# A merged attention and delta-rule stage: first keys and values on another DMA queue, first key block halved, first three query tiles in another order

## The reference, cut to what matters

```python
s = einsum(q_nope, k_nope) + einsum(q_pe, k_pe)        # per query block of 128
p = softmax(where(k_pos <= q_pos, s * scale, -inf))
o = einsum(p, v)
decay = exp(where(causal, g[..., :, None] - g[..., None, :], -inf))
```

## Time and profile before

| | us |
|---|---|
| median of three runs | 2585.17 |
| lowest, highest | 2581.58, 2592.66 |
| time of the profiled execution | 2578.27 |
| its span | 2576.6 |
| TensorE busy in the span | 2331.9 (91%) |
| first DMA of the merged stage issued | at 698.24 |

### The profile page before, as it was taken

The page is one execution under the profiler, slowest core; times in us unless marked ns, Lnnn a source line. Parts: engine busy times, 40 slices in busy tenths (PEclk is TensorE's granted clock), DMA queues, the critical chain, the costliest instruction groups (busy, mean ns, idle before and its releaser), DMA issues. The chain is left out here.

```text
span 2576.6 us, 47589 instructions
## 1 busy us (share of the span) xinstructions
PE 2331.9 (91%) x17494; PEld 1339.2 (52%) x17495; DVE 1074.2 (42%) x2440; ACT 910.1 (35%) x2283; POOL 392.4 (15%) x630
## 2 busy tenths in 40 slices
PE   6999999999688999999999999699985999999990
PEld 2545545455356666666666667355543444444440
DVE  2433334333345665665666566224345222222223
ACT  2263462734545554554545554111110011010112
POOL 1000000000110000000000010133321222222224
PEclk8999999999879999999999999899987999999995
DMA  9112121110353213121221112833321879999787
GB/s 335 72 65 70 52 78 54 56 54 32 107 141 105 75 53 94 56 82 49 80 69 65 51 33 95 294 126 111 131 90 33 238 193 307 273 323 303 225 237 287
DMA packets 187896, 334.49 MB, mean 130 GB/s; under 512 B 19724, under 2 KB 119719, under 8 KB 184503
## 3 DMA queue, kind: packets, MB, share of 16 engines
q1 hardware_dynamic: 173878, 281.51, 32.3%
q0 software_dynamic: 13824, 50.34, 8.1%
HBM read 242.36 MB, written 89.44 MB: 129 GB/s over the span
## 5 line engine op out<-in xcount | busy, mean ns | idle before, releaser
L706 PE MATMUL pV<-mod_rows_then_work,w_in_sb 128*128 128x512 f32 x768 | 341.3, 598 | 4.7 <-DMA w_in_sb<-in_w_in_dram 4.7
L2066 PE MATMUL hidden_ps<-w,keys_values_then_all 128*128 x752 | 331.5, 594 | 1.0 <-SPq L1938 1.0
L1140 ACT ACTIVATE probs<-scores,neg_max 128x512 f32<-128x512 f32 (+3 forms) x320 | 199.5, 624 | 345.6 <-DVE neg_max L1265 228.5
L1417 PE MATMUL scores<-keys_values_then_all,queries 96*128 96x512 f32 (+3 forms) x640 | 309.9, 567 | 7.2 <-DMA keys_values_then_all<-kp_d 7.2
L706 PEld LDWEIGHTS pV<-mod_rows_then_work,w_in_sb 128*128 128x128 f32 x768 | 145.0, 191 | 178.2 <-issue 177.5
L2066 PEld LDWEIGHTS hidden_ps<-w,keys_values_then_all 128*128 128x128 f32 x752 | 143.2, 191 | 181.5 <-issue 181.5
L1715 PE MATMUL out_ps<-keys_values_then_all 128*128 128x512 f32 x512 | 226.2, 600 | 2.5 <-ACT keys_values_then_all L1580 2.5
L1422 PE MATMUL bank<-ident,probs 128*128 128x128 f32 x1088 | 188.7, 290 | 7.0 <-ACT probs L1140 6.7
L1265 DVE TENSOR_REDUCE neg_max<-scores 128x1 f32<-128x512 f32 x192 | 132.2, 688 | 131.7 <-PE scores L1417 131.1
L1434 PE MATMUL outT_ps<-probs_T,keys_values_then_all 128*64 128x128 f32 x2176 | 160.0, 287 | 27.3 <-issue 23.1
L1996 ACT ACTIVATE keys_values_then_all<-hidden_ps 128x256 f32<-128x256 f32 x47 | 18.0, 384 | 455.5 <-PE hidden_ps L2066 455.5
(11 more groups left out here) (368 smaller groups left out, 3317.3 us busy)
## 6 DMA issues: line engine op xcount, KB each, us to landing
w<-in_w_dram SPq DMA_DIRECT2D x64, 1024.0 KB, 10.3
w_sb<-in_w_dram SPq DMA_DIRECT2D x32, 1024.0 KB, 14.4
w_mod_rows<-in_w_mod_dram SPq DMA_DIRECT2D x16, 1024.0 KB, 5.0
kqv<-qkv_d SPq DMA_DIRECT2D x16, 768.0 KB, 4.3
mod_rows_then_work<-in_w_mod_dram SPq DMA_DIRECT2D x4, 2048.0 KB, 14.9
x_in<-in_x_dram SPq DMA_DIRECT2D x16, 512.0 KB, 4.2
qkv_d<-l_out SPq DMA_DIRECT2D x32, 256.0 KB, 2.3
keys_values_then_all<-y_d SPq DMA_DIRECT2D x16, 512.0 KB, 4.9
```

The lines of the kernel that those rows point to most:

```text
L706: last = pe.matmul(pV[n % 2][:], win[:, k, QKV0 + c * P:QKV0 + (c + 1) * P], hT[:, s % 2, k, :], start=(k == 0), stop=(k == ND - 1))
L1140: act.activation(prob[:, e, 0:w].rearrange("p t k -> p (t k)"), pS[e][:, 0:w * P], ACT.Exp, scale=-1.0, bias=nmin[:, i % 2, h, b:b + 1], a ...
L1417: pe.matmul(pS[e][:, 0:w * P], qT[:, i % 2, slot(h)], kT[:, 4 * b:4 * b + w, slot(h), :], start=True, stop=True).then_inc(s_ready, 1)
L2066: last = pe.matmul(pH[par][:], xT[par][:, k], m.w13[:, ds(slot, 1), k].rearrange("p s n -> p (s n)"), start=(k == 0), stop=(k == ND - 1))
```

## The change

`TILE` begins 1, 3, 0 instead of 3, 0, 1. `KV` gets a border at tile 2. The two load helpers take the issuing engine; groups 0 and 1 (tiles 0 and 1, tiles 2 and 3) are issued by ScalarE ahead of its table load, the others by SyncE as before. SyncE issues the first decay rows ahead of the first q, k, v.

```diff
-TILE = [3, 0, 1] + list(range(4, NT)) + [2]
+TILE = [1, 3, 0] + list(range(4, NT)) + [2]
-    KV = [0, 4, 8, 12, NT]
+    KV = [0, 2, 4, 8, 12, NT]
+        def load_k(eng, n):
+            t, end = KV[n], KV[n + 1]
+            eng.dma_start(kT[0:NOPE, t:end].rearrange("p t (e b) k -> p (t e) (b k)", e=2),
+                          m.kn_d[t * P:end * P, :].rearrange("(e p) n -> p e n", p=NOPE)).then_inc(k_loaded[n], 16)
+            for i in range(t, end):
+                eng.dma_start(kT[NOPE:, i], m.kp_d[i * ROPE:(i + 1) * ROPE, :].unsqueeze(1).to_broadcast([ROPE, AH, P])
+                              ).then_inc(k_loaded[n], 16)
+
+        def load_v(eng, n):
+            t, end = KV[n], KV[n + 1]
+            eng.dma_start(v[:, t:end], m.v_d[t * P:end * P, :].rearrange("(t p) n -> p t n", p=P)).then_inc(v_loaded[n], 16)
...
+            load_g(0)
             load_kq(0)
-            load_g(0)
             load_q(0)
-            load_k(0)
-            load_v(0)
             load_q(1)
...
-                    for s in range(1, len(KV) - 1):
+                    for s in range(2, len(KV) - 1):
                         if i == max(0, KV[s] - 5):
-                            load_k(s)
-                            load_v(s)
+                            load_k(sp, s)
+                            load_v(sp, s)
...
         @block.scalar
         def _(act):
             wait = waiter(act)
+            for n in range(2):
+                load_k(act, n)
+                load_v(act, n)
             act.preload_act_table_set("natural_log_exp_and_others")
```

More of the change, by code:

```diff
@@ L920, in _ @@
             wait = waiter(sp)
[L922 to L932, removed]
             def load_q(i):
```

## The result

Over 22 runs each, the changed kernel takes 2592.74 us (median) and the kernel before 2587.98 us: ratio 1.0019, 95% interval 1.001 to 1.0028. It is 4.9 us slower, well within the 0.5% that the prediction took as no change, but on the other side of the forecast of 7.8 us less, and 0.7 us above the range. The range was built on the median of three runs, 2585.17, and with the ratio on that base the time would be 2590.1, inside it: the direction is what failed, for the interval leaves out 1. The profiled execution after took 2600.46 us, its span is 2598.7. The two profiled executions are not typical of their kernels: that of before lies 9.7 us under its median over 22 runs, that of after 7.7 us over. So of the 22 us between the two traces only 4.9 are the kernels'.

What follows compares the result with a forecast made beforehand. TensorE was taken to bound the stage's long middle, with waits and low clock in its first 102 us. Gains of 2.4 + 2.9 + 2.5 = 7.8 us took 2585.17 to 2577.4, range 2566 to 2592 (8 in 10).

Steps and rivals of the forecast that it cites:

- The opening: Start of the merged stage: first mask at 713.4 instead of 715.82, 2.4 us gained (0.2 to 3.9).
- I take the middle, 705.3: Opening: q, k, v land at 705.3, between 703.1 (ScalarE takes nothing from SyncE) and 707.5 (equal bytes).
- the late bound: Opening: with equal bytes for both queues, q, k, v land at 707.5 and 0.2 us are gained.
- The rows' place ahead of q, k, v gives nothing by itself: Opening: the 2.12 us wait for decays goes, but q, k, v take its place.
- ScalarE's issues: Opening: eight DMA issues take 5.4 us, then a 1.28 us table load; hidden with 0.6 us to spare.
- rival (c): Opening: ScalarE gets stuck issuing, from 1.25 us an issue on; mask 6.5 to 8.7 us later, 2592 to 2594; chance 0.07.
- First combine: First tile's combine no longer waits behind ScalarE's copies: 2.9 us gained (0 to 3.3).
- Clock: Low clock from 745 to 760, behind the first combine's wait, may go: 2.5 us gained (0 to 7.5).
- The new order: Merged stage: 697 of 1664 list places hold another step, same work; 6 us either way through the clock.
- rival (d): Merged stage: the 697 moved steps cost, 6 us, at 2591; chance 0.10 on the losing side alone.
- (a): Opening and combines: q, k, v share equally, the combine's wait reappears elsewhere; 0.2 us gained, 2585; chance 0.25.
- signs of being wrong: ScalarE's issues averaging over 1.25 us, first mask later than 715.8, or windows from 800 on differing more than the opening.

Runs made afterwards that it cites:

- e3: The changed kernel with q, k, v ahead of the decay rows on SyncE again; ratio to before 1.0005.
- e12: The kernel before with the first keys and values (six DMAs) issued by ScalarE, nothing else moved; ratio to before 1.0024.
- e11: The changed kernel with q, k, v ahead of the rows and ScalarE waiting for them to land before its eight loads; ratio to before 1.003.
- e1: The kernel before with the tile order 1, 3, 0 alone, all loads as before; ratio to before 0.9995.
- e10: The kernel before with the first tile's combine moved ahead of the delta-rule steps with ScalarE's copies; ratio to before 0.9992.
- e5: The changed kernel with q, k, v ahead of the rows and ScalarE issuing only the first group's keys; ratio to before 1.0.
- e6: New tile order and halved groups as in the changed kernel, but every load issued by SyncE, q, k, v first; ratio to before 1.0005.
- e4: The kernel before with MIX_LEAD at 1.002 instead of 1.0, same loads and tile order; ratio to before 0.996.

## Why the prediction was wrong, step by step

**The opening (2.4 us gained, bounds 0.2 to 3.9): wrong.** The failed step is where q, k, v land: "I take the middle, 705.3", with 707.5 for equal shares as the late bound. The product started at 708.67, in a stage that began 0.3 us sooner, so 1.5 us beyond the late bound. The middle was taken from no row, and the late bound had two errors. It gave ScalarE's queue and SyncE's the same bytes, 1.05 MB each. Measured were 0.68 and 1.42 MB, since loads issued behind q, k, v moved before these were complete; that the sum of 2.1 MB came out right was luck. And I read the earlier trace rows as if any mixture moved at the rate of that moment; but its fast slices (324 to 403 GB/s) were those led by q, k, v, and in the changed kernel the same slices ran at 154 to 226, so that 2.1 MB took 10.7 us instead of 9.3. Apart from the bounds, "The rows' place ahead of q, k, v gives nothing by itself" missed that it costs beside ScalarE's stream: e3, with that place undone, has the product at 5.3 us instead of 10.8, the mask 2.6 us sooner. The rest of the chain was right: from the product's start to the mask were 8.1 us on paper and 8.07 in the trace. So a mask at +15.2 us was forecast and +18.8 came: 1.2 us lost instead of 2.4 gained.

The Trainium skill's rule ("DMA: Bandwidth & Descriptors", "Issuing engines are not separate DMA queues") was given in the prediction with a gain of 0.2 us; e12 agrees that a second issuer brings no bandwidth: the same DMAs from the other engine, and the last keys come 5.8 us later, not sooner. It should have weighed more than the middle between two bounds, though the gain of 0.2 us that I worked out from it was also too kind.

**ScalarE's issues (hidden, 0.6 us to spare; rival (c) from 1.25 us an issue): half right.** They took 9.0 us with the table load still to come, 1.1 us each, not 0.68; single ones rose to 1.6, where SyncE's had reached 2.32 in a loaded queue. They were hidden all the same, but only since q, k, v were later still: the exponential started 2.7 us later than in before, where the spare was 0.6. e11 uncovers them.

**First combine (2.9 us): VectorE's wait went, TensorE's went in part.** In the changed kernel VectorE waits 0.88 us there instead of 2.85. But the 3.1 us of ScalarE's copies stand now before the exponential of a pair of tile 3, and in e1's trace, as in the changed kernel's, TensorE waits 1.8 us for the last of them, so that "whose products cover more" was half right at best (TensorE, e1):

```profile
739.94 0.60 PE L1422 MATMUL bank<-ident,probs 128*128 128x128 f32 x4
742.38 0.18 PE L1376 MATMUL bank<-Y_blocks,W_U_blocks 32*32 32x32 f32 x1 [1.84 <-ACT Y_blocks L1098]
```

Before, TensorE waited 2.07 and 1.25 us there, so by its waits 1.5 of 3.3 us are gone. e10 makes the move alone and leaves the term anywhere from 0 to 5 us. That the full 2.9 us were not gained is not shown; that the wait partly moved to the next step is.

**Clock (2.5 us): not there in the changed kernel.** From 744 to 762 its three windows of 6 us show 0.73, 0.56 and 0.87, and over the 60 us from 740 on the clock is 0.80 against 0.77. After that wait e1 shows the lower level again, for about as long as in the earlier trace rows:

```profile
744.00:750.00 6.00, 6.00 (x32) 3.95 (x31) 0.90 (x3) 2.02 (x6) 0.00 (x0) 0.50 0.14 46
750.00:756.00 6.00, 6.00 (x19) 3.37 (x18) 2.54 (x7) 0.78 (x2) 0.00 (x0) 0.50 0.00 0
```

But the idea was not empty. e3 walks the same list, its TensorE waits 1.86 us for the same copy at 743.73, and its clock is back much sooner:

```profile
744.00:750.00 6.00, 6.00 (x50) 4.03 (x47) 0.90 (x3) 3.19 (x10) 0.37 (x1) 0.72 0.14 46
750.00:756.00 6.00, 6.00 (x48) 4.52 (x47) 4.26 (x14) 2.02 (x6) 0.00 (x0) 1.00 0.25 68
```

From its first to its second combine are 28.9 us, in e1 35.2; e5 (29.2) and e11 (29.3) are like e3, e6 (35.8) and the changed kernel (35.3) like e1. So kernels that differ in their opening alone can differ by some 6 us in the stretch behind it. e3 loses most of that lead again: 7.4 us ahead of e1 at the third combine, 1.6 at the ninth, 2.6 at the last. What tips it is not shown.

**The new order (within 6 us either way): right in size.** e1 says -1.3 us with 4 either way. (The 24 us behind those 6 are what a clock of 0.97 costs over 800 us, not the length of the low stretches.) That reweaving as such can move the time by more, e4 shows: 10 us. So rival (d) was priced too low, though it was not the cause here.

In sum: forecast -7.8; loads about +6 (changed kernel over e1, with 4.4 either way), order about -1 (with 4 either way), measured +4.9. Of the rivals, (a) came nearest in its mechanism, a shared queue and a wait that reappears, and its price of nothing gained was still too kind. The loads' 6 us are more than the changed kernel's delay against e1 in the traces, 1.8 us at the mask and 3.6 to 4.6 us from the first combine to the last; the difference is within the uncertainty.

Of the prediction's signs of being wrong, the mask later than 715.8 came (716.74). ScalarE's issues stayed under 1.25 us on average. The third, windows from 800 on, these two traces cannot settle: of the 20.5 us between their last combines 7.4 lie ahead of the third, but e1, whose time is not measurably different from before's, is 15.9 us behind it at the last combine as well.

## What to carry to other kernels

A second issuing queue did not add bandwidth to this opening, whose DMA engines were 80% or more busy from the third us on; what it changed is which transfer is late. Before moving loads to it, list what must land first, and leave that alone at the head of the one queue; halve the first group instead (e6 moved the first mask 3.5 us ahead of e1's that way, and kept 2.5 to the stage's end, though its time does not show it). When an order written by a planner is perturbed, measure a neutral perturbation of the same size too: here it was worth twice the change under study.

## What the runs showed of the hardware that I had not expected

A transfer's place in its queue mattered more than the bytes beside it. From the issue of q, k, v (0.79 MB) to the product's start were 4.5 us at the head of the only queue, 5.3 at the head of one of two (e3), and 10.1 behind 0.26 MB of rows with keys on the other queue. In the first case the DMA view has 246 packets for 1.00 MB up to the landing (4.1 KB each), in the last 1113 for 2.11 MB (1.9 KB). So twice the bytes moved, at 196 GB/s instead of 221: most of the delay is what else got in before the end of q, k, v, loads issued behind them in the same queue included, and a smaller part is the rate. That the small pieces lower the rate is my reading; no run changed their size alone. And issues took longer on both engines as more lay in the queues: SyncE's issue of the first rotary queries took 1.21 us instead of 0.58, and ScalarE's rotary keys rose from 0.69 us each for the first two to 1.62 for the next two, and 1.99 in e11.
